# Attention weights scaled before they are transposed, values stationary, in an eight-stage transformer kernel on one core

## The chip, the core and the metric

The kernel runs on one core of one Trainium2 chip. The metric is the device time of one execution in microseconds (us). The time before is the median of three runs, 1513.32 us.

## What is computed

The program is a three-layer transformer over 256 tokens of width 1024: a first block (retention and a small causal attention called moba, then a feed-forward part), a block with a 16-head attention with forget gates (fox), and a block with a 16-head latent attention (mla), each with feed-forward parts, norms and gates around it. All is in fp32. What matters here is the softmax attention that the three share, cut down from the reference:

```python
s = jnp.where(k_pos[None, :] <= q_pos[:, None], s, -jnp.inf)   # s: scores of 128 queries, scaled
w = jax.nn.softmax(s, axis=-1).astype(v.dtype)
o = jnp.einsum('bhqk,bkhd->bqhd', w, v)                        # then o.reshape(B, S, H * D) @ w_o
```

moba has 8 heads of width 64 (with 256 tokens it is plain causal attention), fox 16 heads of width 64, mla 16 heads of width 128. The output of each is multiplied by a weight matrix, so it is needed with the head's features on the partitions (transposed).

## The kernel before

Every dense product is made of fp32r matmuls on split operands: a matrix is divided into a high part (`w_hi`, `xTh`) and the rest (`w_lo`, `xTl`), and three matmuls (high by high, low by high, high by low) give the product. The high part of each weight unit of 128x2048 is made by ScalarE (ACT, `split_to` at L1262), the rest by VectorE (DVE, L1785) or, for the stages in `POOL_STAGES`, by GpSimd (POOL, L499). The attentions themselves are plain fp32.

Five engines run their own programs, written out by hand in order, and wait for each other on counters (`need("pe", "o", name, h)` waits until the instruction marked with that label is done). Nothing is reordered by a scheduler.

Each attention is a software pipeline over heads. Step `s` of TensorE (PE) is: `scores(s)`, `turn(s-1)` (three transposes of the weights of head s-1 into bank 6), `weigh(s-2)` (weights times values into bank 7), and then the pieces of dense work in `fill[s]`. Step `s` of ACT is: its pieces for `fill[s-1]`, `exps(s)`, `turned(s-1)` (copy of bank 6 to SBUF). Step `s` of DVE is: `soft(s)` (mask, scale and row minimum, from the scores' bank), its pieces for `fill[s-1]`, `gather(s-2)`.

In `weigh(h)` the turned weights are stationary and the values move, three matmuls (L865 to L867), and the result has queries on the partitions. `gather(h)` (L2018, L2021) takes the reciprocal of the sums and scales the result out of bank 7 into SBUF. `weigh(h)` first waits for `gather(h-1)`, because both use bank 7 (`take(7, ("o", name, h))`).

Afterwards the outputs are transposed on PE and split into high and rest: for moba after the attention (`to_xT("moba", ...)`, 8 transposes), for fox in steps 11 and 13 and after the attention (16), for mla in `turn_o(g)`, one group of four for every pair of heads g, in steps 4, 6, ... 16 and after the attention (32), with `keep_oT` on ACT and `rest_oT` (L2344) on DVE.

In mla the dense pieces of steps 0 to 12 are the query projections `uq`: a long piece, 18 matmuls `uq(g, (2, 0))`, in step 2g-3, and a short one, 9 matmuls `uq(g, (1,))`, in step 2g-2. DVE rotates the queries in `turn_rope(g)`, four instructions at L2338, in its step 2g-2. In fox the pieces are query and key projections and `fox_v5` (steps 0 to 10) and parts of the output projection (12 to 17); in moba gate projections and the transposes of the retention output (8 of them in step 6).

Of the kernel before, what the change touches and what calls it, by code (L numbers as in the profile page):

```python
# [30 lines left out]
P = 128  # L31
T = 2
# [147 lines left out]
def build(nc, dram, marks):  # L180
# [32 lines left out]
    with ExitStack() as ctx:  # L213
# [17 lines left out]
        cTh = sb("cTh", 3 * S, F32R)[:, :].rearrange("p (k n) -> p k n", k=3)  # L231
        cTl = sb("cTl", 3 * S, F32R)[:, :].rearrange("p (k n) -> p k n", k=3)
        hTh = sb("hTh", 2 * S, F32R)[:, :].rearrange("p (k n) -> p k n", k=2)
        hTl = sb("hTl", 2 * S, F32R)[:, :].rearrange("p (k n) -> p k n", k=2)
# [62 lines left out]
        mo = mqk.rearrange("p (b t) n -> p b t n", b=2)[:, 0]  # L297
# [13 lines left out]
        fo = cf.tiles(T, D)  # L311
# [4 lines left out]
        cq_ = cm(2 * 512)  # L316
        cq = cq_[:, 0:T * QL].rearrange("p (t n) -> p t n", t=T)
        mlo = cq_.rearrange("p (b t n) -> p b t n", b=2, t=T)
# [187 lines left out]
        def site_ready(site, t, q):  # L506

            return {"ret": ("gated", q, t), "moba": ("o", "moba", MOBA_H - 1), "mix": ("ev", f"moba_out{q}", t),
                    "fox": ("o", "fox", 8 * q + 7), "raw": ("ffn_out", 0, t)}.get(site, ("norm", site, t, q))
# [10 lines left out]

        O_BANK = [2, 3, 2, 3, 2, 1, 0, 1]
# [11 lines left out]
        def _(pe):  # L533
# [310 lines left out]
            def attention(name, heads, qk, v, dv, fill):  # L844
# [91 lines left out]
            for i in range(2):  # L936
                for t in range(T):
# [4 lines left out]
                      lambda h, t: mv[:, t, h * MOBA_DH:(h + 1) * MOBA_DH], MOBA_DH,  # L942
# [6 lines left out]
            to_xT("moba", mo, (0,), b0=4)  # L949
            chunk("ret_out1", (0, 1), slot0=8)  # L950
            need_xT("moba", (0,))
            chunk("moba_out0", (0, 1))
            moba_out1 = Chunk("moba_out1", (2, 3))
# [40 lines left out]
            for l in range(2):  # L994
# [55 lines left out]
                if l == 0:  # L1050
# [47 lines left out]
                    def fox_v(h, t):  # L1098
                        need("pe", "ev", f"fox_v{4 + h // 8}", 1)
                        return fv[:, t, h * FOX_DH:(h + 1) * FOX_DH]  # L1100

                    v5 = Chunk("fox_v5", (0, 1))
                    o0, o1 = (Chunk(f"fox_o{c}", b, ready="fox") for c, b in ((0, (0, 1)), (1, (2, 3))))
# [7 lines left out]
                    attention("fox", FOX_H, fox_qk, fox_v, FOX_DH, fill)  # L1111
                    for t in range(T):
                        need("pe", *site_ready("fox", t, 1))
                        transposes(4 + t, ("xT", "fox", t, 1), ("T", "fox", t, 1),
                                   [(j * P, fo[:, t, (4 + j) * P:(5 + j) * P]) for j in range(4)])
# [7 lines left out]
                else:  # L1123
# [35 lines left out]
                    def turn_o(g):  # L1159
                        need("pe", "o", "mla", 2 * g + 1)  # L1160
                        transposes(O_BANK[g], ("oT", g), ("oTf", g),
# [78 lines left out]
        def _(act):  # L1240
# [158 lines left out]
            def attention(name, heads, fill):  # L1399
# [12 lines left out]
                for s in range(heads + 3):  # L1412
# [4 lines left out]
                    if 1 <= s <= heads:  # L1417
                        turned(s - 1)
# [1037 lines left out]
```

## Time and profile before

| | |
|---|---|
| median of three runs | 1513.32 us (1513.23 to 1513.48) |
| span of the profiled execution, first to last instruction | 1511.2 us |
| mean granted TensorE clock | 0.998 |
| PE busy | 1493.9 us, 99% |
| DVE, ACT, POOL busy | 61%, 52%, 13% |

The runs lie about 2.1 us over the span of the profiled execution; this part lies outside the instructions and is taken as unchanged. A busy share of 99% on PE says that there is hardly a gap in its work, but the ends of matmuls are modelled and overlap, so what a piece of work costs on PE is read from the start of one instruction to the start of the next.

### The profile page before, as it was taken

What the parts mean: (1) busy time and instruction counts of PE and PEld (TensorE: products, weight loads), DVE (VectorE), ACT (ScalarE), POOL (GpSimd) and SP (SyncE); (2) the same over time, 40 slices, a digit from 0 to 9 for tenths busy, and PEclk for the clock granted to TensorE, in tenths of its full rate; (3) what the DMA queues carried; (4) which work ended last, traced back from release to release, by engine and by line L of the source; (5) the groups of instructions that cost most, each with busy time, mean ns of one, the idle gap of its engine ahead of it and who ended that gap; (6) DMA issues with size and microseconds to landing.
All of it is one profiled execution on the core that took longest, in us unless ns stands there. A gap on an engine that the chain in (4) does not pass through costs nothing.

```text
span 1511.2 us, 21617 instructions
## 1 busy us (share of the span) xinstructions
PE 1493.9 (99%) x8200; PEld 1293.6 (86%) x8200; DVE 920.0 (61%) x1192; ACT 792.0 (52%) x956; POOL 189.9 (13%) x56
## 2 busy tenths in 40 slices
PE   8999999999999999999999999999999999999997
PEld 6888888888888888898888888888888998888886
DVE  7475465666666566523776668766666455756667
ACT  5446545444444444666554456654446654544456
POOL 0014211000040000362100001000005441100010
PEclk9999999999999999999999999999999999999999
DMA  8545446655546555551565556565555434655562
GB/s 313 182 140 177 160 156 196 212 191 194 193 160 203 194 186 177 174 186 65 187 206 187 194 195 226 175 218 185 185 191 162 123 121 162 205 199 184 187 211 81
DMA packets 187258, 273.71 MB, mean 181 GB/s; under 512 B 10144, under 2 KB 137280, under 8 KB 187200
## 3 DMA queue, kind: packets, MB, share of 16 engines
q1 hardware_dynamic: 183136, 261.72, 51.6%
q10 hardware_dynamic: 4064, 11.18, 2.4%
q8 instruction: 41, 0.67, 0.2%
q14 instruction: 17, 0.14, 0.0%
HBM read 271.78 MB, written 1.05 MB: 181 GB/s over the span
## 4 chain that ended last, share of the span: by engine, by line
PE 94%; DVE 3%; ACT 2%; DMA 1%; issue 0%; SPq 0%; ACTq 0%; DVEq 0%
PE bank L694 23%; PE bank L696 12%; PE bank L551 8%; PE bank L553 7%; PE bank L552 7%; PE acc L551 7%; PE acc L552 7%; PE acc L553 7%; PE bank L726 3%; PE acc L853 2%; PE acc L547 2%; PE bank L608 2%; PE bank L601 2%; PE bank L616 2%; DVE tanh L1869 1%; DVE x L1890 1%
## 5 line engine op out<-in xcount | busy, mean ns | idle before, releaser
L1785 DVE TENSOR_TENSOR w_lo<-w_raw,w_hi 128x2048 fp32r<-128x2048 f32 (+2 forms) x209 | 475.2, 2278 | 163.1 <-ACT w_hi L1344 121.4
L694 PE MATMUL bank<-xT,w_hi 128*128 128x512 f32 x1520 | 380.0, 392 | 0.2 <-DVE w_lo L1785 0.2
L499 POOL TENSOR_TENSOR w_lo<-w_raw,w_hi 128x2048 fp32r<-128x2048 f32 (+1 forms) x41 | 176.7, 4316 | 1278.6 <-ACT w_hi L1262 1278.6
L694 PEld LDWEIGHTS bank<-xT,w_hi 128*128 128x128 f32 x1520 | 276.3, 189 | 52.4 <-DVE w_lo L1785 0.9
L1344 ACT ACTIVATE w_hi<-w_raw 128x2048 fp32r<-128x2048 f32 x145 | 276.4, 1907 | 0.0
L696 PEld LDWEIGHTS bank<-xT,w_lo 128*128 128x128 f32 x1520 | 207.4, 190 | 14.8
L696 PE MATMUL bank<-xT,w_lo 128*128 128x256 f32 x1520 | 211.9, 282 | 0.0
L1262 ACT ACTIVATE w_hi<-w_raw 128x2048 fp32r<-128x2048 f32 (+3 forms) x106 | 190.9, 1817 | 21.2 <-DMA w_raw<-in_w_in 11.4
L551 PE MATMUL acc<-w_hi,hTh 128*128 128x512 f32 x400 | 156.2, 391 | 0.0
L552 PE MATMUL acc<-w_lo,hTh 128*128 128x512 f32 x400 | 156.2, 391 | 0.0
L553 PE MATMUL acc<-w_hi,hTl 128*128 128x512 f32 x400 | 155.6, 389 | 0.0
L551 PE MATMUL bank<-w_hi,xT 128*128 128x512 f32 (+1 forms) x336 | 132.3, 394 | 0.0
L553 PE MATMUL bank<-w_hi,xT 128*128 128x512 f32 (+1 forms) x336 | 129.6, 386 | 0.0
L552 PE MATMUL bank<-w_lo,xT 128*128 128x512 f32 (+1 forms) x336 | 129.1, 384 | 0.0
L1355 ACT ACTIVATE squares<-bank 128x512 f32<-128x512 f32 x50 | 29.9, 598 | 140.5 <-PE bank L696 140.5
L1366 ACT ACTIVATE hTh<-hid 128x512 fp32r<-128x512 f32 x45 | 28.4, 632 | 136.3 <-PE acc L553 136.3
L2011 DVE CUSTOM_DVE_ANT_0 arena<-acc,mask 128x128 f32<-128x128 f32 x80 | 25.4, 356 | 115.2 <-PE acc L853 115.2
L553 PEld LDWEIGHTS acc<-w_hi,hTl 128*128 128x128 f32 x400 | 75.1, 188 | 16.0
L551 PEld LDWEIGHTS acc<-w_hi,hTh 128*128 128x128 f32 x400 | 75.3, 188 | 14.3
L552 PEld LDWEIGHTS acc<-w_lo,hTh 128*128 128x128 f32 x400 | 75.3, 188 | 13.7
L1355 ACT ACTIVATE tanh<-bank 128x512 f32<-128x512 f32 x45 | 26.8, 596 | 106.8 <-PE bank L696 106.8
L551 PE MATMUL bank<-xT,w_hi 128*128 128x256 f32 x271 | 78.5, 290 | 0.0
(220 smaller groups left out, 2092.9 us busy)
## 6 DMA issues: line engine op xcount, KB each, us to landing
w_raw<-in_ffn_w_in SPq DMA_DIRECT2D x176, 512.0 KB, 4.4
w_raw<-in_ffn_w_out SPq DMA_DIRECT2D x88, 512.0 KB, 4.1
w_raw<-in_w_in SPq DMA_DIRECT2D x52, 512.0 KB, 4.6
w_raw<-in_fox_w_in SPq DMA_DIRECT2D x24, 512.0 KB, 4.5
w_raw<-in_w_ffn_gate SPq DMA_DIRECT2D x22, 512.0 KB, 4.4
w_raw<-in_w_ffn_up SPq DMA_DIRECT2D x22, 512.0 KB, 4.2
w_raw<-in_w_ffn_down SPq DMA_DIRECT2D x22, 512.0 KB, 4.1
w_raw<-in_ple_w_gate SPq DMA_DIRECT2D x16, 512.0 KB, 4.5
```

The lines of the kernel that those rows point to most:

```text
L499: pool.tensor_tensor(w_lo[s][:, 0:cols], w_raw[u % RING][:, 0:cols], w_hi[s][:, 0:cols].bitcast(F32), ALU.subtract).then_inc(w_lo_done[u % ...
L547: mm = pe.matmul(bank[b][:, c:c + P], src, ident, is_transpose=True, start=True, stop=True)
L551: pe.matmul(out, ah, bh, start=first, stop=False, skip_group_check=biased)
L552: pe.matmul(out, ah, bl, start=False, stop=False, skip_group_check=biased)
L553: return pe.matmul(out, al, bh, start=False, stop=last, skip_group_check=biased)
L694: pe.matmul(out, wh[:, k, m], both, start=k == 0, stop=False)
L696: mm = pe.matmul(out[:, S:], wl[:, k, m], xTh[:, k], start=False, stop=k == KD - 1)
L726: mm = pe.matmul(out, (xTl if part == 1 else xTh)[:, k, tok], both[:, k], start=part == 0 and k == 0, stop=last and k == KD - 1)
L1262: nc.scalar.activation(hi, raw, ACT.Copy).then_inc(w_hi_done, 1)
L1344: nc.scalar.activation(w_hi[slots[u]][:, :], w_raw[u % RING][:, :], ACT.Copy).then_inc(w_hi_done, 1)
L1355: nc.scalar.activation(dst.rearrange("p (m n) -> p m n", m=2), low[:, b:b + 2, S:], ACT.Copy)\
L1785: nc.vector.tensor_tensor(w_lo[s][:, 0:cols], w_raw[u % RING][:, 0:cols], w_hi[s][:, 0:cols].bitcast(F32), ALU.subtract).then_inc(w_lo_don ...
```

## The change

The scaling by the reciprocal sums moves from the attention's output to its weights: `weights(h)` on DVE, directly behind `soft(h)`, waits for the exponentials of the same head and scales them in SBUF, in place; `turn(h)` on PE waits for that. In `weigh(h)` the values are stationary now and the turned weights move: two matmuls, of 256 and of 128 columns. The result has features on the partitions, so the transposes of the outputs go away. `keep_o(h)` (ACT, at the end of its step h+2) copies the high part of bank 7 to `xTh` or `sTh`, and `rest_o(h)` (DVE, at the start of its step h+3) writes the rest and frees bank 7. The head's rows are picked by `head_place`: for heads of width 64 the matmul computes two heads' values and half of the rows is used.

```diff
-                need("pe", "exp", name, h)
+                need("pe", "weights", name, h)
                 transposes(6, ("pT", name, h), ("PT", name, h),
                            [(c * P, pr[:, h % 2, c * P:(c + 1) * P]) for c in range(3)])
...
                 take(7, ("o", name, h))
                 need("pe", "pT", name, h)
-                b, p = bank[7], pT[:, h % 2]
-                pe.matmul(b[:, 0:dv], p[:, 0:P], v(h, 0), start=True, stop=True)
-                pe.matmul(b[:, dv:2 * dv], p[:, P:2 * P], v(h, 0), start=True, stop=False)
-                pe.matmul(b[:, dv:2 * dv], p[:, 2 * P:3 * P], v(h, 1), start=False, stop=True)\
+                out, p = bank[7][:, 0:S], pT[:, h % 2]
+                pe.matmul(out, v(h, 0), p[:, 0:S], start=True, stop=False)
+                pe.matmul(out[:, P:S], v(h, 1), p[:, S:S + P], start=False, stop=True)\
...
-            to_xT("moba", mo, (0,), b0=4)
...
-                    fill |= {11: [lambda: to_xT("fox", fo, (0,), tiles=(0,))], 12: [lambda: o0.run(0, tiles=(0,), part=0)],
-                             13: [lambda: to_xT("fox", fo, (0,), tiles=(1,)), lambda: o0.run(0, tiles=(0,), part=1)], 14: [lambda: o0.run(0, tiles=(1,))],
+                    fill |= {12: [lambda: o0.run(0, tiles=(0,), part=0)],
+                             13: [lambda: o0.run(0, tiles=(0,), part=1)], 14: [lambda: o0.run(0, tiles=(1,))],
...
-                    for g in range(7):
-                        fill[2 * g + 4].append(lambda g=g: turn_o(g))
...
+                def keep_o(h):
+                    need("act", "PV", name, h)
+                    rows, k = head_place(name, h)
+                    dst = (sTh if name == "moba" else xTh)[rows, k, :]
+                    go(("oh", name, h), dst, bank[7][rows, 0:S])
...
                     if 1 <= s <= heads:
                         turned(s - 1)
+                    if 2 <= s < heads + 2:
+                        keep_o(s - 2)
...
-                def gather(h):
-                    need("dve", "PV", name, h)
+                def weights(h):
+                    need("dve", "exp", name, h)
                     s, r = 2 * (h % 4), 2 * (h % 2)
                     did(nc.vector.reciprocal(rsum[:, r:r + 2], psum_e[:, s:s + 2]))
                     settle()
                     for t in range(T):
-                        did(nc.vector.tensor_scalar(out(h, t), bank[7][:, t * dv:(t + 1) * dv],
-                                                    rsum[:, r + t:r + t + 1], None, ALU.mult),
-                            *(("o", name, h) if t else ()))
+                        c = slice(0, P) if t == 0 else slice(P, 3 * P)
+                        did(nc.vector.tensor_scalar(pr[:, h % 2, c], pr[:, h % 2, c], rsum[:, r + t:r + t + 1], None,
+                                                    ALU.mult),
+                            *(("weights", name, h) if t else ()))
+
+                def rest_o(h):
+                    need("dve", "oh", name, h)
+                    rows, k = head_place(name, h)
+                    hi, lo = (m[rows, k, :] for m in ((sTh, sTl) if name == "moba" else (xTh, xTl)))
+                    did(nc.vector.tensor_tensor(lo, bank[7][rows, 0:S], hi.bitcast(F32), ALU.subtract), "o", name, h)
...
                 for s in range(heads + 3):
+                    if s >= 3:
+                        rest_o(s - 3)
                     if s < heads:
                         soft(s)
+                        weights(s)
                     for work in fill.get(s - 1, ()):
                         work()
-                    if 2 <= s < heads + 2:
-                        gather(s - 2)
```

The order on DVE, in mla, in a step with `turn_rope` (L2338 before, L2327 now) and up to the first instruction of the next step's `soft` (L2011 before, L1995 now). Before:

```order
L2011 ISA arena,negmax<-acc,mask 128x128 [waits act_done,pe_done]
L2011 ISA negmax 128x1
L2011 ISA arena,negmax<-acc,mask 128x256
L2011 ISA negmax 128x1
L2338 TENSOR_TENSOR arena<-bank,arena 64x256 x4
L2018 RECIPROCAL exp_rsum<-exp_sum 128x2 [waits pe_done]
L2021 TENSOR_SCALAR arena<-acc,exp_rsum 128x128 [waits dve_done]
L2021 TENSOR_SCALAR arena<-acc,exp_rsum 128x128
L2011 ISA arena,negmax<-acc,mask 128x128 [waits act_done,pe_done]
```

And of the change:

```order
L1995 ISA arena,negmax<-acc,mask 128x128 [waits pe_done]
L1995 ISA negmax 128x1
L1995 ISA arena,negmax<-acc,mask 128x256
L1995 ISA negmax 128x1
L2002 RECIPROCAL exp_rsum<-exp_sum 128x2 [waits act_done]
L2006 TENSOR_SCALAR arena<-arena,exp_rsum 128x128 [waits dve_done]
L2006 TENSOR_SCALAR arena<-arena,exp_rsum 128x256
L2327 TENSOR_TENSOR arena<-bank,arena 64x256 x4
L2014 TENSOR_TENSOR xT<-acc,xT 128x256 [waits act_done]
L1995 ISA arena,negmax<-acc,mask 128x128 [waits pe_done]
```

The reciprocal and the two scalings stand ahead of the four rotations and wait for ACT now; the instruction that frees bank 7 (L2014, `rest_o`) stands behind the rotations, where the scalings stood that freed it before.

The order on PE at the same place, from the scores (L853) of the step after, by way of the transposes of the weights (L547) and `weigh` (L865 and on), to the next dense piece (L551). Before, where the four transposes behind `weigh` are `turn_o` of an even step:

```order
L853 MATMUL acc<-arena 128x128 x2
L853 MATMUL acc<-arena 128x256 x2
L547 MATMUL acc<-ident,arena 128x128 [waits act_done]
L547 MATMUL acc<-ident,arena 128x128 x2
L865 MATMUL acc<-arena 128x128 [waits dve_done]
L866 MATMUL acc<-arena 128x128
L867 MATMUL acc<-arena 128x128
L547 MATMUL bank<-ident,arena 128x128 x4
L551 MATMUL bank<-xT,w_hi 128x256 [waits w_lo_done1]
```

And of the change:

```order
L853 MATMUL acc<-arena 128x128 x2
L853 MATMUL acc<-arena 128x256 x2
L547 MATMUL acc<-ident,arena 128x128 [waits act_done,dve_done]
L547 MATMUL acc<-ident,arena 128x128 x2
L865 MATMUL acc<-arena 128x256 [waits dve_done]
L866 MATMUL acc<-arena 128x128
L551 MATMUL bank<-xT,w_hi 128x256 [waits w_lo_done0]
```

The transposes of the outputs are gone, three matmuls have become two, and the transposes of the weights wait for DVE beside ACT.

## Rows read from the trace of the kernel before

**Rows 1.** The page: busy time of PE, and the chain that ended last.

```profile
PE 1493.9 (99%) x8200; PEld 1293.6 (86%) x8200; DVE 920.0 (61%) x1192; ACT 792.0 (52%) x956; POOL 189.9 (13%) x56
...
PE 94%; DVE 3%; ACT 2%; DMA 1%; issue 0%; SPq 0%; ACTq 0%; DVEq 0%
```

**Rows 2.** PE's waits: who waited for whom, us in total, times, longest.

```profile
PE bank L601 <- DVE xT L1825: 0.4, 1, 0.4
```

**Rows 3.** Timeline of PE in mla, steps 4 to 6: start us, us, instruction, count.

```profile
1198.68 0.49 PE L547 MATMUL acc<-ident,arena 128*128 128x128 f32 x3
1199.01 0.39 PE L865 MATMUL acc<-arena 128*128 128x128 f32 x2
...
1199.68 0.60 PE L547 MATMUL bank<-ident,arena 128*128 128x128 f32 x4
...
1201.19 1.47 PE L853 MATMUL acc<-arena 128*128 128x128 f32 x8
1202.50 0.49 PE L547 MATMUL acc<-ident,arena 128*128 128x128 f32 x3
```

**Rows 4.** Timeline of DVE in the same stretch (in brackets the idle time before).

```profile
1198.88 0.29 DVE L2011 CUSTOM_DVE_ANT_0 arena<-acc,mask 128x128 f32<-128x128 f32 x1 [2.65 <-PE acc L853]
...
1199.44 1.77 DVE L2338 TENSOR_TENSOR arena<-bank,arena 64x256 f32<-64x256 f32 x4
1201.25 0.17 DVE L2018 RECIPROCAL exp_rsum<-exp_sum 128x2 f32<-128x2 f32 x1
1201.45 0.61 DVE L2021 TENSOR_SCALAR arena<-acc,exp_rsum 128x128 f32<-128x128 f32 x2
```

**Rows 5.** Timeline of ACT in the same stretch.

```profile
1199.56 0.40 ACT L1270 ACTIVATE arena<-arena,negmax 128x128 f32<-128x128 f32 x1 [2.04 <-DVE negmax L2011]
...
1200.36 0.19 ACT L1270 ACTIVATION_READ_ACCUMULATOR arena<-arena,negmax 128x1 f32 x1
```

**Rows 6.** Groups of DVE by shape: count, busy us, mean ns of one, idle before.

```profile
L2169 DVE TENSOR_SCALAR arena<-arena,mean_var,rsqrt_y 128x256 f32<-128x256 f32 x8 | 2.7, 410 | 0.0
L2275 DVE TENSOR_TENSOR cTl<-acc,cTh 128x256 fp32r<-128x256 f32 x2 | 0.8, 424 | 1.8 <-ACT arena L1270 1.8
L2295 DVE TENSOR_SCALAR decay<-decay 16x256 f32<-16x256 f32 x1 | 0.3, 281 | 0.0
```

**Rows 7.** Timeline of PE in moba, steps 6 and 7.

```profile
164.03 0.49 PE L547 MATMUL acc<-ident,arena 128*128 128x128 f32 x3
164.35 0.33 PE L865 MATMUL acc<-arena 128*128 128x64 f32 x2
...
164.97 1.05 PE L547 MATMUL bank<-ident,arena 128*128 128x128 f32 x8
...
166.51 0.49 PE L547 MATMUL acc<-ident,arena 128*128 128x128 f32 x3
```

**Rows 8.** Timeline of DVE in the same stretch of moba.

```profile
164.79 1.28 DVE L1825 TENSOR_TENSOR xT<-bank,xT 128x512 fp32r<-128x512 f32 x2
```

**Rows 9.** Timeline of PE in fox, steps 11 and 12.

```profile
699.84 0.82 PE L853 MATMUL acc<-arena 128*128 128x128 f32 x4
700.97 0.52 PE L547 MATMUL acc<-ident,arena 128*128 128x128 f32 x3 [0.32 <-ACT arena L1270]
```

**Rows 10.** Timeline of DVE in fox, steps 15 and 16.

```profile
713.45 2.29 DVE L1785 TENSOR_TENSOR w_lo<-w_raw,w_hi 128x2048 fp32r<-128x2048 f32 x1
```

**Rows 11.** Timelines of DVE and of POOL around 89 us.

```profile
89.18 4.59 DVE L2133 TENSOR_SCALAR rsqrt_v<-rsqrt_b 128x32 f32<-128x32 f32 x1
...
88.82 4.90 POOL L499 TENSOR_TENSOR w_lo<-w_raw,w_hi 128x2048 fp32r<-128x2048 f32 x1 [85.79 <-ACT w_hi L1262]
```

**Rows 12.** Busy time by stretch (moba, fox, mla): stretch, us, then PE, PEld, DVE, ACT, POOL with counts.

```profile
126.00:181.00 55.00, 55.00 (x297) 46.96 (x296) 22.40 (x66) 31.20 (x60) 27.14 (x6) 1.00 0.48 163
650.00:723.00 73.00, 72.23 (x497) 65.47 (x496) 26.58 (x117) 44.80 (x104) 27.50 (x6) 1.00 0.35 120
1184.00:1267.00 83.00, 83.00 (x571) 76.43 (x571) 41.86 (x154) 45.45 (x107) 30.61 (x9) 1.00 0.37 123
```

More of the change, by code:

```diff
@@ L506, in site_ready, with head_place @@
         def site_ready(site, t, q):
-            return {"ret": ("gated", q, t), "moba": ("o", "moba", MOBA_H - 1), "mix": ("ev", f"moba_out{q}", t),
-                    "fox": ("o", "fox", 8 * q + 7), "raw": ("ffn_out", 0, t)}.get(site, ("norm", site, t, q))
+            return {"ret": ("gated", q, t), "mix": ("ev", f"moba_out{q}", t),
+                    "raw": ("ffn_out", 0, t)}.get(site, ("norm", site, t, q))
+        def head_place(name, h):
+            if name == "mla":
+                return slice(0, P), h
+            return slice(64 * (h % 2), 64 * (h % 2) + 64), h // 2 + (8 if name == "fox" else 0)
         TURN_BANK = {4: (4, 5, 6, 7), 8: (4, 5, 6, 7), 5: (6, 7, 0, 1)}
@@ L519, in build @@
         LAST_BANK = [3, 2]
-        O_BANK = [2, 3, 2, 3, 2, 1, 0, 1]
         def q_bank(g):
@@ L840, in ffn, with attention @@
                 note(("ffn_full", f, 1, 1), "w_used", u + 2)
-            def attention(name, heads, qk, v, dv, fill):
+            def attention(name, heads, qk, v, fill):
                 def scores(h):
@@ L1106, in _ @@
                         fill[3 + n] = [lambda n=n: v5.run(n // 2, tiles=(n % 2,))]
-                    fill |= {11: [lambda: to_xT("fox", fo, (0,), tiles=(0,))], 12: [lambda: o0.run(0, tiles=(0,), part=0)],
-                             13: [lambda: to_xT("fox", fo, (0,), tiles=(1,)), lambda: o0.run(0, tiles=(0,), part=1)], 14: [lambda: o0.run(0, tiles=(1,))],
+                    fill |= {12: [lambda: o0.run(0, tiles=(0,), part=0)],
+                             13: [lambda: o0.run(0, tiles=(0,), part=1)], 14: [lambda: o0.run(0, tiles=(1,))],
                              15: [lambda: o1.run(0, tiles=(0,))], 16: [lambda: o1.run(0, tiles=(1,), part=0)],
                              17: [lambda: o1.run(0, tiles=(1,), part=1)]}
[L1111 to L1115, printed above, removed]
+                    attention("fox", FOX_H, fox_qk, fox_v, fill)
                     turn_p(0)
@@ L1157, in uq @@
                                 note(("qnf", g), "w_used", u + 1)
-                    def turn_o(g):
-                        need("pe", "o", "mla", 2 * g + 1)
-                        transposes(O_BANK[g], ("oT", g), ("oTf", g),
-                                   [(j * S + t * P, mlo[:, g % 2, t, j * VD:(j + 1) * VD])
-                                    for t in range(T) for j in range(2)])
                     def mla_qk(h, t):
@@ L1185, in _ @@
                     oa = [unit_steps(f"mla_oa{c}", (3, 2)) for c in range(2)]
-                    fill[13] += [lambda: [need("pe", "oT", g) for g in range(4)], oa[0][0]]
+                    fill[13] += [lambda: need("pe", "o", "mla", 7), oa[0][0]]
                     fill[15].append(oa[0][1])
@@ L1197, in _ @@
                     turn_p(1)
-                    need("pe", "oT", 6)
-                    need("pe", "oT", 7)
+                    need("pe", "o", "mla", 15)
                     ob0.run(1, tiles=(0,))
@@ L1410, in turned @@
                     go(("pT", name, h), pT[:, h % 2], bank[6][:, 0:3 * P])
+                def keep_o(h):
[3 more added lines that the diff above has]
+                    go(("oh", name, h), dst, bank[7][rows, 0:S])
+                    if name == "fox" and h % 8 == 7:
+                        for t in range(T):
+                            note(("xTh", "fox", t, h // 8), "act_done", counts["act_done"])
                 for s in range(heads + 3):
@@ L1659, in _ @@
                     fill[0].append(lambda: keep_q(1))
-                    for g in range(7):
-                        fill[2 * g + 4].append(lambda g=g: keep_oT(g))
                     for g in range(2, 8):
@@ L1996, in ffn, with attention @@
                 return finish
-            def attention(name, heads, out, dv, fill):
+            def attention(name, heads, fill):
                 def soft(h):
@@ L2351, in _ @@
                     fill = {s: [] for s in range(MLA_H + 2)}
-                    for g in range(7):
-                        fill[2 * g + 4].append(lambda g=g: rest_oT(g))
                     for g in range(2, 8):
@@ L2359, in _ @@
                     fill[17].append(lambda: ahead("mla_oa1"))
-                    attention("mla", MLA_H, lambda h, t: mlo[:, (h // 2) % 2, t, (h % 2) * VD:(h % 2 + 1) * VD], VD, fill)
-                    rest_oT(7)
+                    attention("mla", MLA_H, fill)
                     split_to(unit_at["mla_ob1"][1] + 1)
```

60 lines of the change are left out of this document (19 added, 41 removed).

## The prediction

> **What bounds the kernel now.** First the busy shares: PE has 1493.9 of 1511.2 us, and the chain that ended last is 94% PE [rows 1]. So PE's program is the clock: an instruction taken off it is a gain, and any wait put on it is a loss, unless PE already waited there. Second, the list of PE's waits: in the moba attention the only one is 0.4 us, for the rest of the transposed retention output [rows 2]; fox shows one of 0.3 us behind an exponential [rows 9], mla none. ACT and DVE are half idle, but what counts is how late their results come, not how busy they are. So third, the timelines of PE, DVE and ACT at one place in each attention, read from start to start [rows 3 to 10]. The sum is made against the profiled execution (1511.2 us of span, and the runs lie 2.1 us over it) and is then added to the median, 1513.3. About 0.2%, 3 us, is what a measurement can tell from no change: 1510.3 to 1516.3.
>
> **What goes.** Three transposes of 128 columns take 0.33 from their start to the next matmul (1198.68 to 1199.01), so 0.11 each [rows 3]. 56 transposes of outputs go (moba 8, fox 16, mla 32): 6.2 us. With those of fox go waits around them. The scores of step 11 start at 699.84 and are half of mla's, which take 1.31 (1201.19 to 1202.50) [rows 3], so 0.65; the next transposes should start at 700.49 and start at 700.97, 0.48 late, 0.32 of it shown as idle [rows 9]. I take three times this, 1.4 us, for steps 11 to 14 and the tail.
>
> **What `weigh` costs.** Three matmuls before: 0.67 in mla (1199.01 to 1199.68) [rows 3], 0.62 with 64 columns (164.35 to 164.97) [rows 7]. Now 256 and 128 columns: fp32 scores of 128 + 128 + 256 + 256 columns take 1.31, so by columns 0.65 for 384 of 768. mla gains 16 x 0.02 = 0.3; the narrow heads pay, by these rows, 0.03, and since half of the computed rows are thrown away I take 0.06 for the loss of the smaller loads: 24 x 0.06 = 1.4 (fox 1.0, moba 0.5, rounded).
>
> **The new chain behind the scores.** Call the start of PE's next instruction after the scores of head h T0. In mla step 4 it is 1198.68 [rows 3]. DVE starts `soft` 0.20 later, at 1198.88 [rows 4]; the exponentials end with the accumulator read at 1200.36 + 0.19, T0 + 1.87 [rows 5]. Before, only the transposes of the next step waited for that. Now comes the reciprocal (0.04 for the handover, which is DVE's own gap between 1201.21 and 1201.25; the scaling starts 0.20 behind it [rows 4]): first scaling at T0 + 2.11. Scalings of this kind, 128 and 256 columns in SBUF, are not in the trace. A scaling by pointers in SBUF of 256 columns takes 0.41 [rows 6], two of 128 columns out of PSUM span 0.61 [rows 4]. I take 0.60 for the pair. The lower bound is half a cycle per column: an SBUF scaling by constants of 256 columns takes 0.28 [rows 6], then 0.45 for the pair. PE may turn at T0 + 2.79 (0.08 for the handover, chosen).
>
> What covers that on PE: `turn` 0.33, `weigh` 0.65, the dense piece, and the next scores. In mla that is 2.29 without a piece, in fox 1.63. So where a piece stands, 1.15 or more, it is hidden; where none stands, it is not:
> - mla: 14 to 15, 2.79 - 2.29 = 0.5; the first `turn`, behind a short piece and scores alone (1.15 + 1.31), 0.3.
> - fox: step 11, 2.79 - 1.63 = 1.16; step 13, which has a short piece since its transposes are gone, 0.3.
> - moba: step 6, whose piece is 8 transposes (0.88): 2.79 - (0.33 + 0.68 + 0.88 + 0.65) = 0.25. Its first step I charge like mla's, 0.3.
>
> **Bank 7.** `weigh(h)` still waits until head h-1 has left bank 7. Before, that was freed by two scalings in the step of its own `weigh`. Now `rest_o(h-1)` stands at the start of DVE's next step but one, behind `soft`, the wait for the exponentials, the scalings, and DVE's dense work. In mla's even DVE steps that work is `turn_rope`, 1.77 us [rows 4]: scalings done at T0 + 2.71, rotations at T0 + 4.42 (issued 0.06 early), `rest_o` by 0.42 (the same operation of 256 columns [rows 6]) at T0 + 4.78, PE free at T0 + 4.86. PE wants it after `turn`, `weigh`, the short piece, scores, `turn`. Its scores of step 4 end at 1198.68 and `turn` of step 5 at 1202.50 + 0.33, T0 + 4.15 [rows 3]; without the four output transposes (0.44) T0 + 3.70. Stall 1.16, in the six odd steps 3 to 13: 7.0 us. Where a long piece stands, or DVE has no dense work, it is hidden. The same wait adds 0.1 at mla's step 15 and 0.1 at fox's. In moba, DVE's two rests of the retention output, 1.28 [rows 8], stand in the way: free at 2.71 + 1.28 + 0.36 + 0.08 - 0.06 = T0 + 4.4; PE there at 2.79 + 0.33 = 3.12; +1.24. In fox step 16 DVE splits a weight unit, 2.29 [rows 10]: 2.71 + 2.29 + 0.36 = 5.36 against 4.16 (0.33 + 0.68 + 2.1 of o piece and scores + 0.33, and what the late transposes add), +1.2. What queues behind a late `weigh` on PE is the dense piece and the next scores; DVE and ACT then wait for those and catch up, so nothing is carried on.
>
> On ACT `keep_o` is the last thing in its step and adds 0.4 to a row of work with over 1 us idle before each exponential (2.04 [rows 5]): nothing, and `turned` goes ahead of it.
>
> **The sum.** mla: 7.0 + 0.3 + 0.6 - 3.5 - 0.3 = +4.1. moba: 0.3 + 0.25 + 1.24 - 0.9 + 0.5 = +1.4. fox: 1.16 + 0.3 + 0.2 + 1.2 - 1.8 + 1.0 - 1.4 = +0.7. Together +6.2: 1519.5 us. With the pair of scalings at 0.45 each stall is 0.15 shorter, about 12 stalls: 1.8 less, 1517.7.
>
> **The rivals.**
> *Faster.* The bank 7 wait does not bite: mla's `rest_o` comes 1.16 us earlier, by T0 + 3.70. It would need the rotations or the exponentials to be that much shorter. Then 7.0 + 1.24 + 1.2 go: -3.2, 1510.1 us; with the chain's waits gone too, -6.4, 1507. Against it: 1.77 of rotations are a row, and nothing else stands between. Chance 0.06.
>
> *Half the stalls.* The scalings are cheap, the handovers short, and before's hidden gaps around the output transposes were larger than I take. Within 3 us of before, about 1515. Chance 0.12.
>
> *Collision with POOL.* A `TENSOR_SCALAR` of only 128x32 on DVE took 4.59 us from 89.18, and ended when a weight split on POOL, 88.82 to 93.72, ended [rows 11]. If the new scalings in SBUF are held like that, each that meets one waits on average half of 4; POOL is busy 27.1 + 27.5 + 30.6 = 85 of 211 us in the attentions [rows 12], so 16 of 40 heads meet one, 2.0 us each, and PE's cover takes half: +14 on the mere chain, less what falls into stalls counted above, about 1530 us. It decides if more than one in five of the scalings lasts over 2 us. For it speaks that row; against it, the scaling by pointers at 0.41 for 256 columns [rows 6] runs at one column per cycle like the operation on PSUM (0.42), and not at the rate of the constants' 0.28. Chance 0.12.
>
> The Trainium skill, "SBUF — State Buffer", section "Who interferes with whom", says that a tensor_scalar inside SBUF can enter a mode with two ports, that the second pair is shared with GpSimd, and that whoever issues first locks the other out for the whole instruction. "VectorE: DVE Perf Modes", "What auto-detection actually checks", counts every single-source operation with both ends in SBUF in. By these pages every new scaling would be both the faster kind (1517.7) and exposed (the collision). The trace agrees for the constants (0.28, and 4.59 beside POOL) [rows 6, 11] and disagrees for the scaling by pointers (0.41) [rows 6]; the new ones take pointers, so I go with 0.41.
>
> **How the numbers follow.** The forecast has 0.70: 1519.5, alone from 1515 (stalls a third shorter, cheap scalings) to 1525 (bank 7 stalls a third longer). Of it 0.06 lies under 1516.3. Faster 0.06; same 0.12 + 0.06 = 0.18; slower 0.76. The range 1513 to 1527 leaves out the faster rival and most of the collision.
>
> **What the profile of the changed kernel would show.** PE waits of `weigh` (L865) for DVE's `rest_o` (L2014): six in mla of about 1.2, one each in moba and fox. Waits of the transposes of weights (L547) for DVE's scalings (L2006) at steps 11 of fox, 6 of moba, 15 of mla. L2006 at about 0.41 for 256 columns: 0.28 means the cheap kind, and single ones of 2 to 5 us mean the collision. `weigh` 0.65 from start to start. PE's busy time falls by about 6 us less what the wider `weigh` costs, while the span grows. Wrong I would be if mla's waits were absent, if `soft` started late (DVE held by its own waits for exponentials), or if the dense stages outside the attentions moved.

## The result and the profile after

The changed kernel takes 1544.74 us (median of five, 1541.99 to 1545.59), the kernel before 1513.39 in the same comparison: a ratio of 1.0203, 95% interval 1.0192 to 1.0214. It is 31 us slower. The forecast was 1519.5, range 1513 to 1527: the sign was right, and four fifths of the loss were not in it.

The page of the changed kernel, busy time and the chain, answers to [rows 1]:

```profile
PE 1499.6 (97%) x8064; PEld 1290.5 (84%) x8064; DVE 956.2 (62%) x1218; ACT 799.0 (52%) x982; POOL 190.0 (12%) x56
...
PE 85%; DVE 10%; ACT 4%; issue 1%; DMA 0%; ACTq 0%; DVEq 0%; SPq 0%
```

PE has 136 records of matmuls fewer and is still "busy" 6 us longer; the chain now spends 10% on DVE, where it spent 3%. The list of PE's waits (us in total, times, longest) answers to [rows 2]:

```profile
PE acc L547 <- DVE arena L2006: 17.1, 12, 5.0
PE acc L865 <- DVE xT L2014: 8.3, 7, 1.6
...
PE acc L865 <- DVE sTl L2014: 1.0, 1, 1.0
```

The second and third lines are the bank 7 wait that was forecast: 9.3 us in 8 waits, 9.6 in the forecast. The first is the wait of the transposes for the scalings, 17.1 us where the forecast had about 3. The groups of DVE by shape say why (count, busy us, mean ns of one, idle before):

```profile
L2006 DVE TENSOR_SCALAR arena<-arena,exp_rsum 128x128 f32<-128x128 f32 x40 | 31.6, 789 | 1.4
...
L2006 DVE TENSOR_SCALAR arena<-arena,exp_rsum 128x256 f32<-128x256 f32 x40 | 22.4, 559 | 0.0
```

The narrow scaling has the longer mean, 789 ns. That can't be work. The view of its tile gives the spread, shortest, median and longest in ns:

```profile
L2006 DVE TENSOR_SCALAR arena<-arena,exp_rsum x80: 285/345/4608, 133.8 to 1281.2; 128x128 f32<-128x128 f32 x40, 128x256 f32<-128x256 f32 x40
```

Two timelines of moba side by side, DVE and then POOL:

```profile
137.41 0.17 DVE L2002 RECIPROCAL exp_rsum<-exp_sum 128x2 f32<-128x2 f32 x1 [2.47 <-ACT arena L1253]
137.61 7.06 DVE L2006 TENSOR_SCALAR arena<-arena,exp_rsum 128x128 f32<-128x128 f32 x2
144.59 0.28 DVE L1995 CUSTOM_DVE_ANT_0 arena<-acc,mask 128x128 f32<-128x128 f32 x1
...
135.43 9.09 POOL L494 TENSOR_TENSOR w_lo<-w_raw,w_hi 128x2048 fp32r<-128x2048 f32 x2 [4.67 <-ACT w_hi L1245]
```

POOL splits two units, 135.43 to 144.52. The first scaling starts at 137.61 and lasts 2.53 (until about the seam of the two splits), the second 4.61, until 144.67, 0.15 behind the end of the second split. The same picture stands at 683.74 in fox (7.39 for the pair, POOL 681.94 to 690.98). In all, eleven scalings in nine of the 40 heads are held (two heads of moba, five of fox, two of mla): nine firsts of 2.2 to 2.9 us, and two seconds of 4.6. Each ends within 0.2 us of a split's end. Together they last 28.6 us longer than undisturbed ones. POOL's splits themselves are not longer than before (4722 ns in the mean of 33, 4719 before).

PE at the same place, and the windows around it (from and to, length, then busy us and count of PE, PEld, DVE, ACT, POOL, then granted clock, DMA share, GB/s):

```profile
140.26 0.82 PE L853 MATMUL acc<-arena 128*128 128x128 f32 x4
144.73 0.90 PE L547 MATMUL acc<-ident,arena 128*128 128x128 f32 x3 [3.64 <-DVE arena L2006]
145.42 1.06 PE L865 MATMUL acc<-arena 128*128 128x256 f32 x2
146.28 0.63 PE L866 MATMUL acc<-arena 128*128 128x128 f32 x2
146.56 0.77 PE L551 MATMUL bank<-w_hi,xT 128*128 128x512 f32 x1
...
153.88 0.82 PE L853 MATMUL acc<-arena 128*128 128x128 f32 x4
...
134.00:140.00 6.00, 5.87 (x28) 4.71 (x27) 3.49 (x8) 5.56 (x9) 4.57 (x1) 1.00 0.22 84
140.00:144.00 4.00, 1.08 (x6) 0.60 (x4) 4.00 (x2) 0.00 (x0) 4.00 (x2) 0.93 0.70 216
144.00:150.00 6.00, 5.27 (x15) 4.42 (x16) 2.35 (x9) 3.54 (x7) 1.32 (x2) 0.50 0.62 206
150.00:154.00 4.00, 4.00 (x19) 3.23 (x19) 0.00 (x0) 0.69 (x1) 3.81 (x1) 0.97 0.00 0
```

A second loss stands behind the first: after the gap the granted clock is 0.50, which is 1.2 of 2.4 GHz, until about 150. Three transposes take 0.69 from start to start, not 0.33, and the dense piece of 24 matmuls 7.32 (146.56 to 153.88) where the same one in the next step takes 5.55. An estimate of what this costs in all: PE's busy time times one minus the granted clock, summed over windows of 2 us in the attentions, makes 6.9 us. This is also why PE's busy time rose although it has less to do: with POOL's work cut (experiment 5) the clock stays up, and the same matmuls make PE busy for 1488.5 us and not 1499.6.

What was forecast is there too. DVE and then PE in mla, an odd step, answer to [rows 3, 4]:

```profile
1214.51 0.29 DVE L1995 CUSTOM_DVE_ANT_0 arena<-acc,mask 128x128 f32<-128x128 f32 x1 [1.72 <-PE acc L853]
...
1216.41 0.55 DVE L2006 TENSOR_SCALAR arena<-arena,exp_rsum 128x128 f32<-128x128 f32 x2
1216.87 1.77 DVE L2327 TENSOR_TENSOR arena<-bank,arena 64x256 f32<-64x256 f32 x4
1218.68 0.42 DVE L2014 TENSOR_TENSOR xT<-acc,xT 128x256 fp32r<-128x256 f32 x1
...
1214.31 0.49 PE L547 MATMUL acc<-ident,arena 128*128 128x128 f32 x3
...
1217.68 0.49 PE L547 MATMUL acc<-ident,arena 128*128 128x128 f32 x3
1219.15 0.70 PE L865 MATMUL acc<-arena 128*128 128x256 f32 x2 [0.99 <-DVE xT L2014]
```

With T0 = 1214.31 the first scaling starts at T0 + 2.10 (forecast 2.11), `rest_o` ends at T0 + 4.79 (forecast 4.78), and PE loses 1.14 from `turn` to `weigh` (1.47 less the usual 0.33; forecast 1.16).

Where the 31 us arose, by the first scores of each attention and the first and last matmul of the feed-forward parts (start us):

| | moba scores | first L694 | fox scores | mla scores | last L694 |
|---|---|---|---|---|---|
| before | 126.8 | 250.6 | 650.1 | 1183.4 | 1455.7 |
| changed | 127.3 | 263.2 | 662.7 | 1206.5 | 1487.7 |
| added since the mark before | 0.5 | 12.1 | 0.0 | 10.4 | 8.9 |

All but 0.5 of it lies in the three stretches that hold an attention (moba 12.1, fox 10.4, mla 8.9); the 400 us between moba's stretch and fox lose nothing.

### The profile page after: what moved, and what is told of

Read it like the earlier page. It is cut to its first block, busy times and chain, and to the rows that moved or that the text cites. A ratio compares the mean times of both kernels' runs of the same rounds, so it can differ in the third digit from the quotient of the medians.

```text
span 1543.3 us, 21376 instructions
## 1 busy us (share of the span) xinstructions
PE 1499.6 (97%) x8064; PEld 1290.5 (84%) x8064; DVE 956.2 (62%) x1218; ACT 799.0 (52%) x982; POOL 190.0 (12%) x56
## 4 chain that ended last, share of the span: by engine, by line
PE 85%; DVE 10%; ACT 4%; issue 1%; DMA 0%; ACTq 0%; DVEq 0%; SPq 0%
PE bank L694 23%; PE bank L696 12%; PE acc L551 6%; PE acc L552 6%; PE acc L553 6%; PE bank L551 6%; PE bank L553 6%; PE bank L552 6%; PE bank L726 3%; DVE arena L2006 2%; PE bank L601 2%; PE bank L608 2%; PE bank L616 2%; PE acc L547 2%; ACT arena L1253 2%; PE acc L853 1%
## 5 line engine op out<-in xcount | busy, mean ns | idle before, releaser
L694 PE MATMUL bank<-xT,w_hi 128*128 128x512 f32 x1520 | 380.1, 392 | 1.1 <-DVE w_lo L1769 1.1
L694 PEld LDWEIGHTS bank<-xT,w_hi 128*128 128x128 f32 x1520 | 276.2, 189 | 53.5 <-DVE w_lo L1769 2.1
L551 PE MATMUL acc<-w_hi,sTh 128*128 128x512 f32 x400 | 156.3, 391 | 0.0
L552 PE MATMUL acc<-w_lo,sTh 128*128 128x512 f32 x400 | 156.2, 391 | 0.0
L553 PE MATMUL acc<-w_hi,sTl 128*128 128x512 f32 x400 | 155.6, 389 | 0.0
L551 PE MATMUL bank<-w_hi,xT 128*128 128x512 f32 (+1 forms) x320 | 127.7, 399 | 0.0
L553 PE MATMUL bank<-w_hi,xT 128*128 128x512 f32 (+1 forms) x320 | 124.5, 389 | 0.0
L552 PE MATMUL bank<-w_lo,xT 128*128 128x512 f32 (+1 forms) x320 | 124.4, 389 | 0.0
L1349 ACT ACTIVATE sTh<-hid 128x512 fp32r<-128x512 f32 x45 | 28.4, 632 | 136.2 <-PE acc L553 136.2
L553 PEld LDWEIGHTS acc<-w_hi,sTl 128*128 128x128 f32 x400 | 75.1, 188 | 16.0
L551 PEld LDWEIGHTS acc<-w_hi,sTh 128*128 128x128 f32 x400 | 75.3, 188 | 14.3
L552 PEld LDWEIGHTS acc<-w_lo,sTh 128*128 128x128 f32 x400 | 75.3, 188 | 13.7
L551 PE MATMUL bank<-xT,w_hi 128*128 128x256 f32 x271 | 78.5, 289 | 0.0
L1253 ACT ACTIVATE arena<-arena,negmax 128x128 f32<-128x128 f32 x80 | 35.8, 448 | 79.7 <-DVE negmax L1995 79.6
```

What stands on the lines that cost most here:

```text
L551: pe.matmul(out, ah, bh, start=first, stop=False, skip_group_check=biased)
L552: pe.matmul(out, ah, bl, start=False, stop=False, skip_group_check=biased)
L553: return pe.matmul(out, al, bh, start=False, stop=last, skip_group_check=biased)
L694: pe.matmul(out, wh[:, k, m], both, start=k == 0, stop=False)
L1253: nc.scalar.activation(out, in_, func, **kw).then_inc(act_done, mark("act_done", *label))
```

## The experiments

Two theories. **P**: most of the loss is the scalings in SBUF, held by POOL's weight splits, with the low clock behind long stalls; bank 7 is a smaller cost beside it. **R**: the late `rest_o` and the longer chain are the loss, POOL has no part. Times are medians; each ratio is against the kernel before, run beside it (1513.5 to 1513.7 us). A difference between two experiments is one of medians from different comparisons.

**1. The scalings left out** (the outputs are not divided by their sums).

```diff
-                    need("pe", "weights", name, h)
+                    need("pe", "exp", name, h)
...
                         soft(s)
-                        weights(s)
```

> The changed kernel with the reciprocal and the two scalings left out (so its attention outputs are not divided by the sums); PE's transposes of the weights wait for the exponentials alone, as before. Theory P (most of the loss is the scalings in SBUF being held by POOL's weight splits, with a lower TensorE clock behind each long stall; the late rest_o on bank 7 is a second, smaller cost): the 17 us of waits behind the scalings and the slow clock go, the bank 7 stalls in mla shrink from 1.0-1.6 to about 0.4, and the time is 1509 to 1514. Theory R (bank 7 and the longer chain are the loss, POOL has no part): the stalls behind rest_o stay at 9 us, and the time is above 1520. Any slowing of POOL or ACT by the new orientation itself would show as a time above 1520 too.

1508.02 us, ratio 0.9962 (0.9948 to 0.9976). PE's waits for `rest_o` shrink to 0.3 us. So stationary values and outputs that need no transposes gain 5.6 us, and the reciprocal and the 80 scalings cost 36.7, bank 7 included, since without them `rest_o` is early. It fell 1.0 below the expected band, 1509 to 1514. R wanted more than 1520; P holds.

**2. The scalings alone, on the kernel before** (outputs are scaled twice).

```diff
+                def weights(h):
+                    ...  # reciprocal and two scalings, as in the change
...
                         soft(s)
+                        weights(s)
...
-                    need("pe", "exp", name, h)
+                    need("pe", "weights", name, h)
```

> The kernel before with one part of the change alone: reciprocal and the two scalings of the weights in SBUF behind soft, the transposes wait for them; weigh, the scaling out of bank 7 (by the same reciprocals, so outputs are scaled twice), and the output transposes stay. Theory P: the same collisions as in the changed kernel, in heads near a POOL split: 17 us of PE waits plus 5 to 7 us of low clock, 1535 to 1542. Theory R: only the 0.84 us longer chain where no dense piece stands, 1515 to 1518.

1553.64 us, ratio 1.0266 (1.0249 to 1.0283): +40, and 12 over the band of P. Its waits for the scalings:

```profile
PE acc L547 <- DVE arena L2022: 12.6, 8, 4.4
PE acc L865 <- DVE arena L2030: 8.2, 8, 1.8
...
PE bank L601 <- DVE xT L1825: 4.3, 2, 2.2
```

The scalings stand ahead of everything that DVE did before, so the old scaling out of bank 7 (L2030) and the rests of the transposed outputs (L1825) come late as well. The low clock, estimated as above, costs 11.4 us; with these waits that is 36.5 of the 40. Ten scalings in SBUF take 2.1 to 4.6 us, each up to the end of a split. The sign and the mechanism are P's; the size has this second layer.

**3. The same scaling with two pointers**: times the reciprocal, then the maximum with a column of zeros.

```diff
-                        ...tensor_scalar(pr[:, h % 2, c], pr[:, h % 2, c], rsum[:, r + t:r + t + 1], None, ALU.mult)
+                        ...tensor_scalar(pr[:, h % 2, c], pr[:, h % 2, c], rsum[:, r + t:r + t + 1], mask[:, 0:1],
+                                         ALU.mult, ALU.max)
```

> The changed kernel, the scalings with a second operation and a second pointer (times the reciprocal, then the maximum with a column of zeros, which changes nothing). The 128x256 instruction with two pointers in the trace of before took 0.41 us, the new one with one pointer takes 0.35. Theory P1 (the faster rate and the lock go together): 0.41 us each, none over 0.5, no clock loss; the bank 7 stalls of 1.1 in mla remain; 1518 to 1522, near the blind forecast. Theory P2 (every scaling inside SBUF is held by a POOL split whatever its rate): ops of 2 to 5 us remain, 1543 to 1547.

1545.35 us, ratio 1.0211 (1.0194 to 1.0228): no change against the changed kernel, P2 and not P1. All the scalings in one line, shortest, median, longest in ns:

```profile
L2006 DVE TENSOR_SCALAR arena<-arena,exp_rsum,mask x80: 345/406/4617, 133.2 to 1281.0; 128x128 f32<-128x128 f32 x40, 128x256 f32<-128x256 f32 x40
```

This is the run that shows the error of the forecast. Undisturbed, the scaling with two pointers takes 345 ns for 128 columns and 406 for 256: 61 ns for 128 more columns, 0.48 per column, on top of a fixed cost of about 0.28 us. Out of PSUM (experiment 7) it is 351 and 475 ns, 0.97 per column. So the 410 of [rows 6], which looked like the 0.42 of an operation on PSUM, is made of twice the rate and a high fixed cost.

**4. `rest_o` one step earlier**, ahead of DVE's dense work.

```diff
-                    if s >= 3:
-                        rest_o(s - 3)
                     if s < heads:
                         soft(s)
                         weights(s)
+                    if 2 <= s < heads + 2:
+                        rest_o(s - 2)
```

> The changed kernel with rest_o(h) one step earlier on DVE: behind the scalings of step h+2 and ahead of DVE's dense work, where it stood at the start of step h+3. By the rows of the changed kernel 9.3 us of waits on PE are for rest_o: they go, nothing else changes, so 1534 to 1537. Under theory R (all of it is bank 7) the time would fall below 1525.

1540.45 us, ratio 1.0173 (1.0156 to 1.0190): 4.3 us gained of 9.3, so the band of 1534 to 1537 was missed by 3.5. PE's waits:

```profile
PE acc L547 <- DVE arena L2006: 19.1, 12, 5.0
...
PE bank L551 <- DVE arena L2327: 2.5, 5, 0.9
PE bank L551 <- DVE x L1819: 1.5, 1, 1.5
...
PE bank L551 <- DVE w_lo L1769: 0.6, 1, 0.6
```

No wait of `weigh` is left, but 4.6 us of new ones are there, for what DVE does behind `rest_o` (rotations, an addition, a weight split), and 2.0 more behind the scalings. With R the time would be under 1525. R falls.

**5 and 6. POOL's splits cut to 32 columns**, in the changed kernel and in the one before (most low parts of POOL's units are stale).

```diff
+                    cols = 32
                     pool.tensor_tensor(w_lo[s][:, 0:cols], ...)
```

> The changed kernel with every weight split on POOL cut to 32 of its 2048 or 1152 columns (the rest of those low parts is left as it was, so the dense products are off); waits and signals stay. Theory P: the scalings meet nothing, no long stall, no clock loss; what stays are the bank 7 stalls in mla (6 of about 1.0) and the chain where no dense piece stands: 1513 to 1518, against 1545. Theory R: POOL has no part and the time stays near 1545.

> The same cut on the kernel before, as the base for the run above: POOL hardly matters there, 1509 to 1513. The difference of the two is then the change without POOL: both theories of a late rest_o and a longer chain say +4 to +7.

Changed: 1516.07 us, ratio 1.0015 (1.0005 to 1.0025). Before: 1510.79, 0.9981 (0.9972 to 0.9991). Both lie in their bands. Without POOL's splits the change costs 5.3 us; with them 31.4. Of the changed kernel, its scalings and its waits:

```profile
L2007 DVE TENSOR_SCALAR arena<-arena,exp_rsum x80: 285/318/350, 130.0 to 1252.5; 128x128 f32<-128x128 f32 x40, 128x256 f32<-128x256 f32 x40
...
PE acc L866 <- DVE xT L2015: 7.1, 7, 1.1
...
PE acc L548 <- DVE arena L2007: 1.7, 4, 0.9
```

No scaling is over 350 ns, and the waits that are left, 8.1 for bank 7 and 1.7 for the scalings, are the kind that the forecast had priced (9.6 and about 3).

**7. The exponentials in PSUM**: ACT writes them into the scores' bank, DVE scales them from there into SBUF. POOL's splits are whole.

```diff
-   go(("exp", name, h) if t else (), pr[:, h % 2, c], pr[:, h % 2, c], ACT.Exp, ...)
+   go(("exp", name, h) if t else (), bank[4 + h % 2][:, c], pr[:, h % 2, c], ACT.Exp, ...)
...
-   nc.vector.tensor_scalar(pr[:, h % 2, c], pr[:, h % 2, c], rsum[...], None, ALU.mult)
+   nc.vector.tensor_scalar(pr[:, h % 2, c], bank[4 + h % 2][:, c], rsum[...], None, ALU.mult)
...
-                    take(4 + h % 2, ("soft", name, h))
+                    take(4 + h % 2, ("weights", name, h))
```

> The changed kernel, but ACT writes the exponentials into the scores' PSUM bank and DVE scales them from there into SBUF; the scores of head h+2 wait for the scalings of head h. POOL's splits are whole again. Theory P with the lock on operands (a scaling with one side in PSUM leaves the port to POOL): no scaling over 0.6 us, the clock stays up, and bank 7 costs 7 us in mla: 1516 to 1521. If any DVE instruction that writes SBUF is held by POOL: 1540 or more.

1521.55 us, ratio 1.0051 (1.0034 to 1.0068), 0.6 over the band of P. The same head of moba, with POOL at work as in the timeline above:

```profile
137.31 0.74 DVE L2006 TENSOR_SCALAR arena<-acc,exp_rsum 128x128 f32<-128x128 f32 x2
...
135.13 9.19 POOL L494 TENSOR_TENSOR w_lo<-w_raw,w_hi 128x2048 fp32r<-128x2048 f32 x2 [4.67 <-ACT w_hi L1245]
```

The pair takes 0.74 in the middle of POOL's two splits; it took 7.06 with its source in SBUF. For these two instructions only the place of the source has changed; the destination is SBUF in both. In this run 23 of the 80 scalings overlap a split of POOL, and the longest takes 0.48 us.

**8, 9, 10. The order on DVE and the pieces of fox.** All three build on the kernel of experiment 7. In 8, `rest_o` goes behind the scalings of step h+2, and in mla the rotations go ahead of reciprocal and scalings. In 9, DVE also does its dense work first in the steps without a new head. In 10, fox's output projection also starts a step earlier and is cut into four pieces of one size.

```diff
-                    if s >= 3:
-                        rest_o(s - 3)
+                    late = name == "mla" and s < heads
+                    first = late or s >= heads               # 8: first = late
                     if s < heads:
                         soft(s)
+                        if late:
+                            for work in fill.get(s - 1, ()):
+                                work()
                         weights(s)
-                    for work in fill.get(s - 1, ()):
-                        work()
+                    elif first:                              # 9 and 10 alone
+                        for work in fill.get(s - 1, ()):
+                            work()
+                    if 2 <= s < heads + 2:
+                        rest_o(s - 2)
+                    if not first:
+                        for work in fill.get(s - 1, ()):
+                            work()
...
-   12: [o0.run(0, tiles=(0,), part=0)], 13: [o0.run(0, tiles=(0,), part=1)], 14: [o0.run(0, tiles=(1,))],
+   11: [o0.run(0, tiles=(0,), part=0)], 12: [o0.run(0, tiles=(0,), part=1)],
+   13: [o0.run(0, tiles=(1,), part=0)], 14: [o0.run(0, tiles=(1,), part=1)],
```

> The kernel of exp_psum with another order on DVE: rest_o(h) behind the scalings of step h+2, and in mla the four rotations ahead of reciprocal and scalings, in the time in which DVE waits for the exponentials. If bank 7 and the chain are all that is left, both are hidden in mla but where no dense piece stands: level of the run without scalings, 1508.0, plus 1.2 in fox step 11, 0.3 in step 13, 0.5 and 0.3 in mla, 0.3 in moba: 1509 to 1512, faster than the kernel before. If bank 7 was not the reason for the waits of weigh, 1516 to 1521 as in exp_psum.

> The kernel of psum_rope_first, which showed two new waits on PE of 1.5 us (for an addition on DVE) and 0.6 us (for a weight split on DVE) just behind the last heads: there rest_o stood ahead of DVE's dense work and waited for ACT. Here DVE does its dense work first in the steps without a new head. If those waits were on the path, 1512 to 1513; if they only moved a wait that was there anyway, 1514.6 as before.

> psum_fill_first, and fox's output projection starts one step earlier in four pieces of 1.42 (steps 11 to 14; it was two of 1.42 and one of 2.85 in 12 to 14), so that no head of fox is without cover. The wait of 1.2 in step 11 goes and nothing else stalls: 1.0 to 1.4 us under psum_fill_first, so 1511 to 1512. If PE then waits for weights or for ACT's split instead, no gain.

8: 1514.60 us, ratio 1.0007 (0.9997 to 1.0017). The bank 7 waits are gone, but two new ones of 1.5 and 0.6 us stand behind the last heads, so it missed its band by 2.6. 9: 1512.13 us, 0.9991 (0.9982 to 1.0000), they are gone, as expected. 10: 1511.04 us, 0.9982 (0.9973 to 0.9991): 2.5 us faster than the kernel before, a small difference but clear of the interval, and at the lower end of the expected band. Of 33.7 us between it and the changed kernel, 23.2 come from one operand moved to PSUM, 9.4 from the order on DVE, 1.1 from the piece in fox. What PE still waits for the scalings in 10:

```profile
PE acc L547 <- DVE arena L2006: 1.8, 5, 0.5
```

**11. ACT scales**, in SBUF and in place, in the order of 9; DVE makes the reciprocal alone.

```diff
+                        need("act", "recip", name, s)
+                        for t in range(T):
+                            c = slice(0, P) if t == 0 else slice(P, 3 * P)
+                            r = 2 * (s % 2) + t
+                            go(("weights", name, s) if t else (), pr[:, s % 2, c], pr[:, s % 2, c], scale=rsum[:, r:r + 1])
...
-                    (DVE's two scalings)
```

> The order of psum_fill_first, but the scalings are made in SBUF by ACT, in place, and DVE makes the reciprocal alone. Theory P (the port is DVE's and POOL's; ACT is not held): no scaling over 0.6 us, the chain 0.1 to 0.4 us longer than with DVE out of PSUM, 1513 to 1516. If a POOL split held any reader of the weights' buffer in SBUF (memory, not the port), scalings of 2 to 5 us and 1530 or more.

1523.47 us, ratio 1.0064 (1.0050 to 1.0078). The scalings on ACT, and PE's wait for them:

```profile
L1253 ACT ACTIVATE arena<-arena,exp_rsum x80: 401/448/496, 134.2 to 1259.9; 128x128 f32<-128x128 f32 x40, 128x256 f32<-128x256 f32 x40
...
PE acc L547 <- ACT arena L1253: 9.0, 13, 1.8
```

27 of the 80 overlap a split of POOL, and the longest takes 0.50 us: not one is held, so it is not the buffer but DVE's way to it. The time missed its band, 1513 to 1516, by 7: in mla the reciprocal stands behind the rotations on DVE, and ACT waits up to 0.9 us for it, on top of 0.40 and 0.49 for its own two scalings. That part of the expectation was wrong.

**12. POOL's split in four instructions**, in the changed kernel.

```diff
-                    pool.tensor_tensor(w_lo[s][:, 0:cols], ...).then_inc(...)
+                    for q in range(4):
+                        c = slice(q * cols // 4, (q + 1) * cols // 4)
+                        ins = pool.tensor_tensor(w_lo[s][:, c], ...)
+                    ins.then_inc(...)
```

> The changed kernel with one edit on POOL: each weight split is issued as four instructions of a quarter of the columns, one behind the other, with the signal on the last. The scalings stay in SBUF on DVE. Theory P in its strict form (POOL holds the port for one instruction and DVE gets it between two): a scaling is held for at most 1.2 us and on average 0.6, two in a row for twice that; the waits of PE behind the scalings fall from 17 to 3-5 us and the clock stays up, so 1518 to 1526. If POOL keeps the port as long as it has work queued, nothing changes: 1542 to 1547.

1526.32 us, ratio 1.0086 (1.0072 to 1.0100), 0.3 over the band: 18 us of the 31 are back. The scalings and PE's wait for them:

```profile
L2008 DVE TENSOR_SCALAR arena<-arena,exp_rsum x80: 285/346/1409, 131.9 to 1261.7; 128x128 f32<-128x128 f32 x40, 128x256 f32<-128x256 f32 x40
...
PE acc L549 <- DVE arena L2008: 4.6, 7, 1.4
```

The longest is 1.41 us, one quarter of a split (1.38 in the mean), where it was 4.6, one whole split. So DVE is held for one instruction of POOL at a time, and not for as long as POOL has work queued. The mean granted clock is 0.999.

## Why the prediction was wrong

**What failed is one step**: "it runs at one column per cycle like the operation on PSUM (0.42), and not at the rate of the constants' 0.28. Chance 0.12." The words are short for this: from the one duration of a pointer scaling in SBUF [rows 6] a rate was read, and from the rate it was argued that the new scalings would not be held by POOL. Experiment 3 shows that the rate was read wrong (0.48 ns per column and a fixed cost of 0.28 us), and the timelines and experiments 5, 7 and 12 that they are held, 11 of 80. With one size in the trace, the duration could not tell a fixed cost from a rate.

The row that did bear on it, 4.59 us for 128x32 ending with POOL's split [rows 11], was given too little weight, and it was not alone. In the kernel before, eight `SCALAR_TENSOR_TENSOR` of 128x512 with their sources in SBUF take 1.5 to 4.9 us beside a split of POOL, where 0.75 is usual, and each ends 0.55 us behind the end of that split. The longest is in the first line (shortest, median, longest in ns); it starts at 1144.06, and POOL's split is the second:

```profile
L1890 DVE SCALAR_TENSOR_TENSOR x<-tanh,rstd,gb x24: 741/750/4920, 607.4 to 1478.3; 128x512 f32<-128x512 f32 x24
...
1143.25 5.18 POOL L499 TENSOR_TENSOR w_lo<-w_raw,w_hi 128x2048 fp32r<-128x2048 f32 x1 [0.51 <-ACT w_hi L1262]
```

The Trainium skill, "SBUF — State Buffer", "Who interferes with whom", had it right as it stands there, and in "VectorE: DVE Perf Modes", "What auto-detection actually checks", the condition is where source and destination lie, not what the scalar is: the runs agree, 7.06 us with the source in SBUF and 0.74 with it in PSUM.

**A second step failed with it**: "so nothing is carried on". Behind the long waits the granted clock was 0.50, for an estimated 6.9 us, and neither the sum nor any rival had a term for the clock.

**The rival's price was too low as well**: +14 on the mere chain, about 1530 in all, against 1544.7. Its waits came out near the measured ones by luck. It had 16 of 40 heads held for 2.0 us, 32 in all, and half of that on PE (which is 16; the 14 is a slip). Measured are 28.6 us in nine heads, each first scaling for 2.2 to 2.9 and two second ones for 4.6, as POOL had two splits queued; in mla most of POOL's splits are the short ones of 2.6 us and fall beside the scalings. On PE 17.1 us of waits stand behind the scalings, less 1.7 that stay without POOL: 15.4. What the price lacked is the rest: `rest_o` later by 9.3 - 8.1 = 1.2 and the low clock 6.9, together 23.5. The runs give 31.4 - 5.3 = 26.1 for POOL. About 2.6 us have no row of their own, and their cause stays open.

**What was right**: the change without POOL costs +5.3 where the sum had +6.2. The chain of mla is met within 0.02 us at each step, and its bank 7 stall at 1.14 for 1.16 in four of six heads (the other two, behind a held scaling, wait longer); so is fox step 16 (PE idle 1.15 before `weigh`, forecast 1.2), and moba's stall is 0.98 for 1.24. By attention the sum is less good, and that the total fits is in part luck. The stretches of the two kernels with POOL cut differ by 0.8 in moba (forecast 1.4), -0.6 in fox (+0.7) and 4.6 in mla (4.1), and by 0.5 ahead of moba, which nothing in the change explains. Two terms were off and nearly cancel. `weigh` takes 0.57 from start to start where a dense piece comes next (161.96 to 162.53 in moba) and more elsewhere; over all heads, without idle time, the two kernels with POOL cut are level, 24.3 us for 24.6, where the forecast had the change 1.2 dearer. And the transposes that went took about 4.8 us, not 6.2 (those of mla 2.9 for 3.5).

R, the rival after the result, is excluded as the main cause by experiments 4 and 5; as the smaller part, 5 of the 31 us, it is what was forecast.

## What to carry to other kernels

Before a DVE instruction with source and destination in SBUF is put on a critical path, look at what POOL runs at that time: it can be held for the rest of POOL's instruction, and again by the next one that is queued. Three ways out were measured here: the source in PSUM (23 us of 31), POOL's work cut into four instructions (18 us), and the operation on ACT (no scaling held; 21 us, together with the order of experiment 9). What was left came from the order of DVE's work. One duration is a fixed cost plus a rate; without a second size, do not read a rate from it. And look through the trace for every instruction that takes far longer than others of its shape, and for what ends when it ends.

Where PE is the bound, a stall of several microseconds costs more than itself: here the long waits (3.6, 5.0, and 2.3 with 1.0) brought an estimated 7 us of lost clock behind them, and the waits of 1.0 to 1.6 us elsewhere brought none.

## What the runs showed of the hardware that was not expected

- A scaling of 128x128 that takes 0.285 us alone took up to 2.9, and one of 128x256 (0.35 alone) 4.6, beside POOL's subtraction of 128x2048; each ended within 0.2 us of the end of that subtraction. POOL was not slowed (4722 ns for 4719).
- The same scaling with its source in PSUM (0.35 and 0.475 us) was held in none of 80 cases, 23 of them beside a split, nor was ACT's in SBUF (0.40 and 0.49), 27 of 80 beside one.
- A second operation with a pointer of its own makes the scaling about 0.06 us longer at either size (345 for 285 ns, 406 for 348) and changes neither the time per column nor the hold by POOL. Which of the two, operation or pointer, costs it was not told apart.
- fp32 matmuls of 256 and 128 moving columns follow each other at 0.43 and 0.14 us when a dense piece comes next (154.86, 155.29 and 155.43 in moba), less than the scores' rate suggested.
- After PE stood idle for 3.6 us, for 5.0 in fox, and for 2.3 and 1.0 close together in moba, the granted clock was 0.50 (1.2 GHz) for 3 to 7 us; behind the single stalls of 1.0 us in mla it stayed at full, and also behind 1.2 and 1.6 us with 0.5 us of work between them. In experiment 2 it fell to 0.50 behind single gaps of 1.8 to 2.2 us.
